# An MoE layer on one core: four residual scratches and buffers, gathers two blocks ahead

## The chip, the cores and the metric

One core of one Trainium2 chip. The metric is device time in microseconds of one execution; its median over repeated runs is compared. All data is fp32.

## The reference, cut to what matters

One transformer layer for 1024 prompt tokens and 64 sample tokens (D = 1024). First an attention and gMLP sub-layer, whose result is added to x; then a mixture of experts, which is what the change touches:

```python
p_group = softmax(t @ w_router_group + b_router_group)
g_prob, g_idx = top_k(p_group, 1)                    # one of 4 groups
logit_e = (t @ w_router_expert + b_router_expert)[group g_idx]
e_prob, e_idx = top_k(softmax(logit_e), 2)           # two of its 8 experts
weight = g_prob * e_prob / sum(e_prob)
hid = silu(xblk @ w_gate[e]) * (xblk @ w_up[e])      # blocks of 128 token slots, one expert each
yb  = hid @ w_down[e]
y   = zeros(T, D).at[row_token].add(yb * row_weight)
x   = x + gate * y
```

Each token has two slots, so two rows are added to its residual row x, in two different blocks. Both of its experts belong to one group. 2176 slots go to 32 experts (D_EXPERT = 256), 68 on average.

## The kernel before

Three stages follow each other, separated by semaphores on which all engines wait (s_end1, s_end2): projections of nine row tiles; attention, out projection, residual and router for the nine tiles; then the experts. In the second stage SyncE stores for each tile (store_tail, L542) the residual rows x_att into every residual scratch in z_d (L547), and h2, the experts' input, into ffn_input_scratch (L549). Before it loads x_att again for the tile two later it waits until those stores have landed (L652).

**Routing.** VectorE works out the slot of each token, with some help of TensorE, and writes tables of indices, `ids`: for each block b a column with the token of each of the 128 slots (TOKEN), the rows to be written if this is the token's first of two blocks (FIRST), and the output rows if it is its last (PROMPT_ROW, SAMPLE_ROW). An index that is FAR beyond the bound is skipped by the DMA. Two counts of s_tab tell that TOKEN and then all tables are there (L1948, L1961). Meanwhile GpSimd clears xg and acc (L776, L777), and SyncE loads the first four experts' weights.

**The blocks.** Block b < 32 belongs to expert `b % NG * EG + b // NG`, so to group b % 4; NG = 4, EG = 8, NE = 32. Blocks 0 to 31 hold the first 128 slots of each expert. Block 32 (NS = NE + 1 = 33 blocks are always run) takes the 128 slots after those of the first expert that has more, and further ones run in a loop only where there are more (overflow_blocks, L117); here there are none.

- **TensorE**: for block b, transposes of hid (hT4, L1178), gate and up matmuls of block b+1 (gu, L1168; L1173 and L1175), transposes of the tokens of block b+2 (xT4, L1159), then down matmuls of b (down, L1184; L1190). Transposes are recorded at line 853. down(b) waits for VectorE's copy hidT(b) (L1982) and until the down banks of b-1 have been read.
- **SyncE**: loads the 3 MB of weights of block b+4 into the slot of b once down(b) is done (L669 to L671, four slots).
- **ScalarE**: half of the xT copies (L1429), silu (L1436), and the prompt gate times row weight (L1443).
- **VectorE**: for block b, in this order (steady, L2005): hidT(b) (L1982), gate_w (L1988), hidden(b+1) (L1974), xT half of b+2 (L1966), then add_rows(b) (L1991): yb = down bank times gate (L1997), then acc += yb (L2000), which waits for the gather of residual rows of b. What stands behind that add in its queue is hidT(b+1).
- **GpSimd** issues all indirect DMAs. A residual scratch holds the partial sum of a token between its two blocks. For block b it issues, in this order (loop at L803):

```
tokens(b+4)                wait: transposes of block b+2        L783
rows_in(b+1)               wait: scatters of block b-1 landed   L786
first_rows_out(b)          wait: add of block b                 L789
last_rows_out(b), two DMAs (prompt rows, sample rows)           L792, L793
```

There are two scratches, used by even and odd blocks, and two acc buffers. Two consecutive blocks of the same parity may hold the same tokens (group b % 4 has parity b % 2); no two blocks of different parity do. Block 32 may belong to any group, so it gathers twice into acc[0]: from z_d[0] with indices EVEN, ahead of the add of block 31, and from z_d[1] with indices ODD behind the scatters of block 31 (L818 to L821); the group that isn't its own has only indices that are skipped.

Of the kernel before, what the change touches and what calls it, by code (L numbers as in the profile page):

```python
# [135 lines left out]
def build_in(nc, a, o, ctx):  # L136
    def sem(name):
        return nc.alloc_semaphore(name)
# [34 lines left out]
    tok_id = sb("tok_id", [P, NT + 1])  # L173
    TOKEN, EVEN, ODD, FIRST, PROMPT_ROW, SAMPLE_ROW = range(6)
    ids = sb("ids", [P, 6, NB], I32)
    roww = sb("roww", [P, 2, NB])
# [97 lines left out]
    yb = sb("yb", [P, D])  # L274
    gi = sb("gi", [P, 6], I32)
# [24 lines left out]
    idf = sb("idf", [P, NB])  # L300
    odd = sb("odd", [P, MAXOV])
    odd_i = sb("odd_i", [P, MAXOV], I32)
    tokf = sb("tokf", [P, 2, NT + 1])
# [26 lines left out]
    s_lss = sem("latent_square_sums_ready")  # L330
    s_rx = sem("router_exponents_ready")
    s_ry = sem("router_exponentials_ready")
    s_A1 = sem("mix_scale_ready")
# [163 lines left out]

    s_E = sem("expert_one_hots_ready")
    s_rank = sem("ranks_ready")
    s_hot = sem("slot_one_hots_ready")  # L500
    s_tabp = sem("tables_summed")
    s_tab = sem("tables_ready")
    s_gmp = sem("gate_rows_filled")
    s_gmr = sem("gate_rows_read")
    s_wd = [sem(f"expert_weights_loaded{i}") for i in range(SLOTS)]
# [12 lines left out]
    s_yv = sem("down_read")  # L518
    s_acc = [sem(f"residual_rows_gathered{i}") for i in range(2)]
    s_sum = sem("rows_summed")  # L520
    s_zsc = [sem(f"residual_rows_scattered{i}") for i in range(2)]
    s_ysc = sem("output_rows_scattered")
# [30 lines left out]
    def _(sp):  # L553
# [101 lines left out]
        store_tail(sp, LAST)  # L655
        for i in range(2):
            sp.wait_ge(s_st2[f"x2_{i}"], 32 * len(range(i, len(seq), 2)))
        sp.wait_ge(s_st2["h2"], 16 * len(seq))
# [36 lines left out]
    def _(g):  # L695
# [88 lines left out]

        def rows_in(par, z, idx):
            g.indirect_dma_start(acc[:, par], None, z, U(idx), bounds_check=TOK - 1, oob_is_err=False).then_inc(s_acc[par], 16)  # L786

        def first_rows_out(par, z, idx):
            g.indirect_dma_start(z, U(idx), acc[:, par], None, bounds_check=TOK - 1, oob_is_err=False).then_inc(s_zsc[par], 16)  # L789

# [6 lines left out]
        tokens(1, at(TOKEN, 1))  # L797
        rows_in(0, z_d[0], at(TOKEN, 0))
        for b in (2, 3):
# [26 lines left out]
        def overflow(j):  # L826

            for z in z_d:
                first_rows_out(0, z, gi[:, FIRST:FIRST + 1])
            g.wait_ge(s_zsc[0], j * 32 + 16 * (NE // 2))  # L830
            g.sem_inc(s_over, 1)
# [5 lines left out]
            rows_in(0, z_d[0], gi[:, EVEN:EVEN + 1])  # L837
            g.wait_ge(s_acc[0], j * 32 + (16 * (NE // 2 + 2) - 16))
            g.sem_inc(s_over, 1)
            rows_in(0, z_d[1], gi[:, ODD:ODD + 1])  # L840
# [10 lines left out]
    def _(pe):  # L851
# [283 lines left out]
        for v in range(2):  # L1135
# [6 lines left out]
            ins.then_inc(s_gmp, 1)  # L1142
        pe.wait_ge(s_E, 1)
        flat = E[:].rearrange("p t e -> p (t e)")
        mm(psum[0][:, 0:(NT + 1) * NE], tri[:], flat, start=True, stop=True)
        mm(psum[1][:, 0:(NT + 1) * NE], ones[:], flat, start=True, stop=True).then_inc(s_rank, 1)

        for k in range(2):
            pe.wait_ge(s_hot, k + 1)
# [4 lines left out]
        ins.then_inc(s_tabp, 1)  # L1154

# [71 lines left out]
    def _(act):  # L1227
# [185 lines left out]
        for v in range(2):  # L1413
# [3 lines left out]
            act.sem_inc(s_gmr, 1)  # L1417
        act.wait_ge(s_rx, 1)
        do(A(rt[:, 1, :, 0:NG], rt[:, 0, :, 0:NG], ACT.Exp))
        do(A(rt[:, 3, :, 0:1], rt[:, 2, :, 0:1], ACT.Exp))  # L1420
        act.sem_inc(s_ry, 1)

# [50 lines left out]
    def _(dve):  # L1473
# [386 lines left out]
        do(TT(col(2), col(11), col(8), ALU.subtract))  # L1860
        signal(s_rx)
        g4 = bcast(T(4, NG).unsqueeze(3), [P, NTT, NG, EG])
# [3 lines left out]
        do(TT(E[:], E1[:], E2[:], ALU.add))  # L1866
        signal(s_E)

        dve.wait_ge(s_ry, 1)
        do(V.tensor_reduce(col(12), T(1, NG), AXX, ALU.add))  # L1870
# [4 lines left out]

        dve.wait_ge(s_rank, 1)
        do(V.tensor_copy(big2[:], psum[1][:, 0:NTT * NE].rearrange("p (t e) -> p t e", e=NE)))
# [41 lines left out]
        for kk in range(2):  # L1919
# [4 lines left out]
            do(TT(hot, hot, bcast(tokf[:, kk, :].unsqueeze(2), [P, NTT, NB]), ALU.mult))  # L1924
            signal(s_hot)

# [13 lines left out]
        dve.wait_ge(s_tabp, 1)  # L1940
        coded, weight = psum[2][:, 0:NB], psum[2][:, NB:2 * NB]
# [63 lines left out]
        def steady(b, u, nth):  # L2005
# [3 lines left out]
            xT_half(b + 2)  # L2009
            add_rows(b, u % 2, u % 2, nth)  # L2010

        for b in range(SLOTS):
            steady(b, b, 16 * (b // 2 + 1))
        with dve.Fori(0, (NE - 2 * SLOTS) // SLOTS) as i:
            for u in range(SLOTS):
                steady(i * SLOTS + (SLOTS + u), u, i * 32 + (16 * (u // 2) + 48))
        for b in range(NE - SLOTS, NS):
# [4 lines left out]
            if b + 2 < NS:  # L2022
                xT_half(b + 2)
            add_rows(b, b % 2, b % 2, 16 * (b // 2 + 1 + (b == NE)))
        n_ov = dve.value_load(ovf_i[0:1, MAXOV:MAXOV + 1], min_val=0, max_val=MAXOV)
        def overflow(j):
# [4 lines left out]
            gate(b, 0)  # L2031
            add_rows(b, 0, 0, j * 32 + 16 * (NE // 2 + 2))

# [36 lines left out]
```

## Time and profile before

| | us |
|---|---|
| median of 3 runs | 1262.55 |
| the runs | 1262.55, 1269.23, 1247.44 |
| the profiled execution, its own time | 1251.21 |
| its span, first to last instruction | 1249.4 |
| granted TensorE clock, mean | 0.93 |
| busy in the span: TensorE, VectorE, GpSimd, ScalarE | 1082.9, 629.0, 309.6, 267.6 |

The page and the rows below are of the profiled execution. Engines: PE is TensorE (PEld its weight loads), DVE VectorE, ACT ScalarE, POOL GpSimd, SP SyncE; a trailing q is the engine's sequencer, which waits and issues. An indirect DMA's busy time on POOL is its issue alone; "to landing" is from the issue until all of it has been written. What stands in square brackets at a row's end is the idle time before it and what ended it.

### The profile page before, as it was taken

To read this page: it belongs to the slowest core of one execution; us is meant where nothing else is said; L and a number is where in the kernel's file an instruction comes from. 1 tells how busy PE (TensorE), PEld (TensorE's weight loads), DVE (VectorE), ACT (ScalarE), POOL (GpSimd) and SP (SyncE) were. 2 spreads that over 40 slices of the span, in tenths; PEclk is the share of its full clock that TensorE was granted. 3 is DMA by queue.
4 is the path that set the end of the run, shared out by engine and by line. 5 is a ranking of instruction groups with operands and counts; after the bars stand their busy time and mean duration, and the time that the engine had idled before them with its cause. 6 is when DMAs were issued, how large, how long until landed. Compare 5 with 4: busy or idle time off the path is not lost.

```text
span 1249.4 us, 13972 instructions
## 1 busy us (share of the span) xinstructions
PE 1082.9 (87%) x4732; PEld 694.4 (56%) x4732; DVE 629.0 (50%) x1209; ACT 267.6 (21%) x595; POOL 309.6 (25%) x350
## 2 busy tenths in 40 slices
PE   4699999999287989989999994399899988988993
PEld 1245555544154456657666753377677766766772
DVE  2445556554463565566575636725344334433442
ACT  1142232222233223232223201011111111111120
POOL 1122222222401110110110001124345334335443
PEclk9799999999678999999999995599999998998998
DMA  8874443331331122221120116538889887877850
GB/s 323 327 264 163 159 154 142 121 121 44 112 91 60 47 90 100 82 97 52 59 93 1 68 51 265 222 101 327 326 296 351 309 310 282 327 277 286 326 208 25
DMA packets 73200, 220.40 MB, mean 176 GB/s; under 512 B 27172, under 2 KB 30903, under 8 KB 57399
## 3 DMA queue, kind: packets, MB, share of 16 engines
q1 hardware_dynamic: 46000, 189.57, 40.4%
q0 software_dynamic: 23760, 26.81, 6.6%
q10 hardware_dynamic: 3382, 3.32, 0.8%
q8 instruction: 29, 0.48, 0.2%
q14 instruction: 29, 0.23, 0.1%
HBM read 200.04 MB, written 79.34 MB: 224 GB/s over the span
## 4 chain that ended last, share of the span: by engine, by line
PE 60%; DMA 14%; DVE 12%; issue 6%; POOL 4%; ACT 3%; ACTq 0%; DVEq 0%; POOLq 0%; SPq 0%
PE bank L898 14%; DMA out<-acc,ids 10%; PE bank L1056 8%; PE bank L853 7%; PE bank L1173 5%; PE bank L1190 5%; PE bank L1175 5%; PE bank L1007 4%; PE bank L1032 4%; DMA acc<-residual_scratch,ids 2%; PE bank L979 2%; PE bank L881 2%; DMA rope_q<-rope_table 1%; DVE probT L1767 1%; PE bank L1078 1%
## 5 line engine op out<-in xcount | busy, mean ns | idle before, releaser
L898 PE MATMUL bank<-W_in,hT 128*128 128x512 f32 (+3 forms) x432 | 181.9, 575 | 3.4 <-ACTq L1289 3.4
L718 POOL TENSOR_SCALAR st<-st 128x1 f32<-128x1 f32 (+6 forms) x77 | 17.7, 230 | 611.7 <-DVEq L1485 611.7
L1190 PE MATMUL bank<-WD,hidT 128*128 128x512 f32 x264 | 129.5, 637 | 27.8 <-DVE hidT L1982 27.8
L1056 PE MATMUL bank<-W_out,mT 128*128 128x512 f32 (+1 forms) x288 | 138.7, 614 | 2.9 <-DVEq L1479 2.9
L898 PEld LDWEIGHTS bank<-W_in,hT 128*128 128x128 f32 (+1 forms) x432 | 80.1, 188 | 94.8 <-issue 89.2
L1173 PE MATMUL bank<-WG,xT 128*128 128x256 f32 x528 | 122.5, 386 | 1.3 <-ACT xT L1429 0.8
L1175 PE MATMUL bank<-WU,xT 128*128 128x256 f32 x528 | 119.4, 379 | 0.0
L1173 PEld LDWEIGHTS bank<-WG,xT 128*128 128x128 f32 x528 | 99.9, 194 | 14.6 <-ACT xT L1429 1.2
L1175 PEld LDWEIGHTS bank<-WU,xT 128*128 128x128 f32 x528 | 100.5, 190 | 13.5
L1190 PEld LDWEIGHTS bank<-WD,hidT 128*128 128x128 f32 x264 | 51.5, 206 | 83.0 <-issue 79.8
L1032 PEld LDWEIGHTS bank<-vall,probT 128*128 128x128 f32 (+1 forms) x656 | 78.1, 187 | 23.3 <-issue 18.5
L1767 DVE COPY probT<-bank 128x512 f32<-128x512 f32 (+3 forms) x104 | 57.0, 548 | 64.9 <-PE bank L853 57.2
L1056 PEld LDWEIGHTS bank<-W_out,mT 128*128 128x128 f32 (+1 forms) x288 | 53.0, 189 | 62.7 <-issue 54.5
L786 POOL DMA_INDIRECT acc<-residual_scratch,ids x34 | 41.5, 1219 | 186.5 <-DMA out<-acc,ids 157.8
L1007 PE MATMUL bank<-kT,qT 104*128 104x512 f32 (+4 forms) x224 | 86.3, 499 | 0.7 <-ACTq L1383 0.7
L1997 DVE TENSOR_TENSOR yb<-bank,gate_w 128x512 f32<-128x512 f32 x66 | 42.5, 686 | 84.1 <-PE bank L1190 84.1
L1032 PE MATMUL bank<-vall,probT 128*128 128x64 f32 (+1 forms) x656 | 81.2, 269 | 2.9 <-DVEq L1479 2.9
L2000 DVE TENSOR_TENSOR acc<-acc,yb 128x1024 f32<-128x1024 f32 x33 | 40.4, 1225 | 80.1 <-DMA acc<-residual_scratch,ids 79.4
L1443 ACT ACTIVATE gate_w<-gate_m,roww 128x1024 f32<-128x1024 f32 x33 | 37.8, 1148 | 171.4 <-DVE yb L1997 171.4
L719 POOL TENSOR_TENSOR st<-st,mhalf 128x1 f32<-128x1 f32 (+6 forms) x77 | 70.0, 909 | 6.4
L853 PE MATMUL bank<-ident,prob 128*128 128x128 f32 (+2 forms) x328 | 49.2, 276 | 16.4 <-ACT prob L1394 6.8
L1974 DVE TENSOR_TENSOR hid<-sg,bank 128x256 f32<-128x256 f32 x33 | 20.0, 606 | 76.5 <-ACT sg L1436 76.0
(280 smaller groups left out, 1401.7 us busy)
## 6 DMA issues: line engine op xcount, KB each, us to landing
WG<-in_w_gate_e SPq DMA_DIRECT2D x33, 1024.0 KB, 6.7
WU<-in_w_up_e SPq DMA_DIRECT2D x33, 1024.0 KB, 8.9
WD<-in_w_down_e SPq DMA_DIRECT2D x33, 1024.0 KB, 12.4
ada_w<-in_w_ada SPq DMA_DIRECT2D x24, 1024.0 KB, 7.4
residual_scratch<-x_att SPq DMA_DIRECT2D x16, 512.0 KB, 3.4
kbuf<-k_scratch SPq DMA_DIRECT2D x12, 384.0 KB, 5.3
xbuf<-in_x_prompt SPq DMA_DIRECT2D x8, 512.0 KB, 3.7
W_in<-in_w_in SPq DMA_DIRECT2D x2, 2048.0 KB, 17.8
```

The costliest lines, as they stand in the source:

```text
L719: g.tensor_tensor(dst, dst, mhalf[:dst.shape[0], 0:dst.shape[1]], ALU.pow).then_inc(s_rs, 1)
L786: g.indirect_dma_start(acc[:, par], None, z, U(idx), bounds_check=TOK - 1, oob_is_err=False).then_inc(s_acc[par], 16)
L853: tr = lambda out, in_, r: nc.tensor.transpose(out, in_, ident[:r, :r])
L898: ins = mm(ps[:R, 0:n], hT[:, t % 2, k, :R], W_in[:, k, c0:c0 + n], start=(k == 0), stop=(k == KD - 1))
L1007: ins = mm(out[:R, 0:m], qT[:depth, s % 2, h, :R], kT[:depth, h, k0 + c0:k0 + c0 + m], start=True, stop=True)
L1032: ins = mm(psum[7][:R, h * VD:(h + 1) * VD], probT[:r, u % 2, b, :R], vall[:r, slot0(t) + b, h * VD:(h + 1) * VD], start=(b == 0), stop=(b ...
L1056: ins = mm(psum[6][:R, :], mT[:, k, :R], W_out[:, k, half * 512:(half + 1) * 512], start=(k == 0), stop=(k == KD - 1))
L1173: mm(psum[2][:, 0:DE], xT[:, k, :], WG[:, slot, k, :], start=(k == 0), stop=(k == KD - 1))
L1175: ins = mm(psum[3][:, 0:DE], xT[:, k, :], WU[:, slot, k, :], start=(k == 0), stop=(k == KD - 1))
L1190: ins = mm(psum[5 + half][:], hidT[:, k, :], WD[:, slot, k, half * 512:(half + 1) * 512], start=(k == 0), stop=(k == 1))
L1767: ops.append(V.tensor_copy(probT[:, u % 2, 4 * j:4 * j + len(full), :R], src[:, 0:len(full), :R]))
L1997: V.tensor_tensor(yb[:, c], psum[5 + half][:], gate_w[:, par, c], ALU.mult).then_inc(s_yv, 1)
```

## The change

One residual scratch and one acc buffer for each expert group, so four of each. Block b uses scratch, buffer and semaphores b % 4. The gather of residual rows is issued two blocks ahead (rows_in(b+2) in the step of block b; blocks 0 and 1 before the loop), and waits for the scatters of block b-2, the last before it in the same buffer. The scratch it reads was last written by block b-2, four blocks before b+2. last_rows_out(b) has a new wait, for the output scatters of block b-1. Block 32 gathers from all four scratches, one after another, each waiting for the landing of the one before: the first in the step of block 30, the second in that of 31, the third and fourth in its own, the fourth also behind the landing of block 31's scatter. The tables EVEN and ODD become four, one for each group. The second stage stores each residual tile four times instead of two. Some semaphores are joined (those of the routing stage), with the same waits.

```diff
-    z_d = [nc.dram_tensor(f"residual_scratch{i}", (TOK, D), F32).ap() for i in range(2)]
+    z_d = [nc.dram_tensor(f"residual_scratch{i}", (TOK, D), F32).ap() for i in range(NG)]
-    acc = sb("acc", [P, 2, D])
+    acc = sb("acc", [P, NG, D])
...
-                sp.wait_ge(s_st2[f"x2_{s % 2}"], 32 * (s // 2))
+                sp.wait_ge(s_st2[f"x2_{s % 2}"], 16 * NG * (s // 2))
...
         tokens(1, at(TOKEN, 1))
-        rows_in(0, z_d[0], at(TOKEN, 0))
+        rows_in(0, 0, at(TOKEN, 0))
+        rows_in(1, 1, at(TOKEN, 1))
...
-            if b:
-                g.wait_ge(s_zsc[(b - 1) % 2], 16 * ((b - 1) // 2 + 1))
-                g.wait_ge(s_ysc, 32 * b)
-            if b + 1 < NE:
-                rows_in((b + 1) % 2, z_d[(b + 1) % 2], at(TOKEN, b + 1))
-            if b + 1 == NE:
-                rows_in(0, z_d[0], at(EVEN, NE))
+            if b >= 2:
+                g.wait_ge(s_zsc[(b - 2) % NG], 16 * ((b - 2) // NG + 1))
+                g.wait_ge(s_ysc, 32 * (b - 1))
+            if b + 2 < NE:
+                rows_in((b + 2) % NG, (b + 2) % NG, at(TOKEN, b + 2))
+            if b + 2 >= NE and b + 2 - NE < NG:
+                group = b + 2 - NE
+                if group:
+                    g.wait_ge(s_acc[0], 16 * (NE // NG + group))
+                rows_in(0, group, at(GROUP + group, NE))
+            if b == NE:
+                g.wait_ge(s_zsc[NG - 1], 16 * (NE // NG))
+                g.wait_ge(s_acc[0], 16 * (NE // NG + NG - 1))
+                rows_in(0, NG - 1, at(GROUP + NG - 1, NE))
             g.wait_ge(s_sum, b + 1)
             if b < NE:
-                first_rows_out(b % 2, z_d[b % 2], at(FIRST, b))
-            last_rows_out(b % 2, at(PROMPT_ROW, b), at(SAMPLE_ROW, b))
-            if b + 1 == NE:
-                g.wait_ge(s_zsc[1], 16 * (NE // 2))
-                g.wait_ge(s_acc[0], 16 * (NE // 2 + 1))
-                rows_in(0, z_d[1], at(ODD, NE))
+                first_rows_out(b % NG, b % NG, at(FIRST, b))
+            if b:
+                g.wait_ge(s_ysc, 32 * b)
+            last_rows_out(b % NG, at(PROMPT_ROW, b), at(SAMPLE_ROW, b))
...
-        do(V.tensor_copy(odd_i[:], ovf[:, 0:MAXOV]))
-        do(TS(odd_i[:], odd_i[:], 1, None, ALU.bitwise_and))
-        do(V.tensor_copy(odd[:], odd_i[:]))
+        do(V.scalar_tensor_tensor(ovg[:], thr[:], float(-NG), ovf[:, 0:MAXOV], ALU.mult, ALU.add))
...
-        do(STT(ids[:, EVEN, NE:], odd[:], FAR, idf[:, NE:], ALU.mult, ALU.add))
-        do(TS(odd[:], odd[:], -FAR, FAR, ALU.mult, ALU.add))
-        do(TT(ids[:, ODD, NE:], odd[:], idf[:, NE:], ALU.add))
+        for group in range(NG):
+            do(TS(other[:], ovg[:], float(group), FAR, ALU.not_equal, ALU.mult))
+            do(TT(ids[:, GROUP + group, NE:], other[:], idf[:, NE:], ALU.add))
...
-            add_rows(b, u % 2, u % 2, nth)
+            add_rows(b, u % 2, u, nth)
```

## Rows read from the trace of the kernel before

**Rows 1.** The page, part 4: shares of the chain that ended last, by line.
```profile
PE bank L898 14%; DMA out<-acc,ids 10%; PE bank L1056 8%; PE bank L853 7%; PE bank L1173 5%; PE bank L1190 5%; PE bank L1175 5%; PE bank L1007 4%; PE bank L1032 4%; DMA acc<-residual_scratch,ids 2%; PE bank L979 2%; PE bank L881 2%; DMA rope_q<-rope_table 1%; DVE probT L1767 1%; PE bank L1078 1%
```

**Rows 2.** Who waited for whom after 860 us: total us, times, longest us.
```profile
POOL acc L786 <- DMA out<-acc,ids: 157.8, 25, 12.3
...
DVE acc L2000 <- DMA acc<-residual_scratch,ids: 79.4, 24, 11.3
...
PE bank L1190 <- DVE hidT L1982: 27.8, 7, 6.4
```

**Rows 3.** Timeline of GpSimd: start us, us, instruction, idle before it.
```profile
866.34 0.97 POOL L793 DMA_INDIRECT out<-acc,ids  x1 [0.30 <-PE bank L853]
...
878.39 0.97 POOL L793 DMA_INDIRECT out<-acc,ids  x1 [0.30 <-issue]
...
893.02 1.00 POOL L786 DMA_INDIRECT acc<-residual_scratch,ids  x1 [12.31 <-DMA out<-acc,ids]
894.32 1.01 POOL L789 DMA_INDIRECT residual_scratch<-acc,ids  x1 [0.30 <-issue]
...
896.93 0.97 POOL L793 DMA_INDIRECT out<-acc,ids  x1 [0.30 <-issue]
...
1132.52 0.97 POOL L793 DMA_INDIRECT out<-acc,ids  x1 [0.30 <-issue]
```

**Rows 4.** Timeline of TensorE: hidden transposes and down projections, same columns.
```profile
835.17 0.38 PE L853 MATMUL bank<-ident,hid 128*128 128x128 f32 x2
...
905.22 5.94 PE L1190 MATMUL bank<-WD,hidT 128*128 128x512 f32 x8 [4.71 <-DVE hidT L1982]
...
1041.02 0.38 PE L853 MATMUL bank<-ident,hid 128*128 128x128 f32 x2
...
1098.20 0.38 PE L853 MATMUL bank<-ident,hid 128*128 128x128 f32 x2
...
1199.92 3.60 PE L1190 MATMUL bank<-WD,hidT 128*128 128x512 f32 x8
...
1214.79 0.38 PE L853 MATMUL bank<-ident,hid 128*128 128x128 f32 x2
...
1225.35 0.38 PE L853 MATMUL bank<-ident,hid 128*128 128x128 f32 x2
1228.59 3.70 PE L1190 MATMUL bank<-WD,hidT 128*128 128x512 f32 x8 [2.86 <-DVE hidT L1982]
```

**Rows 5.** Time to landing between 835 and 1200 us: of scatter L793, then of gather L786.
```profile
DMA to landing us min/median/max: 2.2/7.3/13.8
...
DMA to landing us min/median/max: 3.2/9.3/11.3
```

**Rows 6.** Window: us, PE, PEld, DVE, ACT, POOL busy, clock, DMA share, GB/s.
```profile
911.20:978.00 66.80, 66.80 (x297) 50.84 (x296) 32.60 (x42) 12.77 (x18) 29.04 (x27) 1.00 0.92 348
```

**Rows 7.** DMA issues, 911 to 979 us: count, KB each, median us to landing.
```profile
WD<-in_w_down_e SPq DMA_DIRECT2D x6, 1024.0 KB, 12.2
```

**Rows 8.** The chain of the tail, in order of time.
```profile
1233.66 3.19 DMA acc<-residual_scratch,ids
```

**Rows 9.** Timeline of all engines, end of attention and routing.
```profile
751.04 0.79 SPq L547 DMA_DIRECT2D residual_scratch<-x_att  x2
...
756.60 0.32 SPq L549 DMA_DIRECT2D ffn_input_scratch<-h  x1
...
763.18 0.20 DVE L1730 TENSOR_TENSOR logits<-bank,b_r 128x36 f32<-128x36 f32 x1 [3.78 <-PE bank L1078]
...
765.35 1.80 POOL L777 MEMSET acc<- 128x2048 f32 x1
...
769.26 0.20 DVE L1857 TENSOR_SCALAR rt<-rt 128x72 f32<-128x72 f32 x1
...
806.05 0.17 DVE L1960 TENSOR_TENSOR ids<-odd,idf 128x16 int32<-128x16 f32 x1
...
810.88 0.69 DVE L1966 COPY xT<-bank 128x512 f32<-128x512 f32 x1 [4.66 <-PE bank L853]
```

More of the change, by code:

```diff
@@ L173, in build_in @@
     tok_id = sb("tok_id", [P, NT + 1])
-    TOKEN, EVEN, ODD, FIRST, PROMPT_ROW, SAMPLE_ROW = range(6)
-    ids = sb("ids", [P, 6, NB], I32)
+    TOKEN, FIRST, PROMPT_ROW, SAMPLE_ROW, GROUP = range(5)
+    KINDS = GROUP + NG
+    ids = sb("ids", [P, KINDS, NB], I32)
     roww = sb("roww", [P, 2, NB])
@@ L300, in build_in @@
     idf = sb("idf", [P, NB])
-    odd = sb("odd", [P, MAXOV])
-    odd_i = sb("odd_i", [P, MAXOV], I32)
+    ovg = sb("ovg", [P, MAXOV])
+    other = sb("other", [P, MAXOV])
     tokf = sb("tokf", [P, 2, NT + 1])
@@ L495, in scores @@
         return 2 * (u % 2)
[L498 to L501, printed above, removed]
+    s_hots = sem("routing_exponents_then_expert_then_slot_one_hots_ready")
+    s_sums = sem("ranks_then_tables_summed")
     s_tab = sem("tables_ready")
     s_gmp = sem("gate_rows_filled")
-    s_gmr = sem("gate_rows_read")
+    s_gmr = sem("gate_rows_read_then_router_exponentials_ready")
     s_wd = [sem(f"expert_weights_loaded{i}") for i in range(SLOTS)]
@@ L518, in build_in @@
     s_yv = sem("down_read")
-    s_acc = [sem(f"residual_rows_gathered{i}") for i in range(2)]
+    s_acc = [sem(f"residual_rows_gathered{i}") for i in range(NG)]
     s_sum = sem("rows_summed")
-    s_zsc = [sem(f"residual_rows_scattered{i}") for i in range(2)]
+    s_zsc = [sem(f"residual_rows_scattered{i}") for i in range(NG)]
     s_ysc = sem("output_rows_scattered")
@@ L656, in _ @@
         for i in range(2):
-            sp.wait_ge(s_st2[f"x2_{i}"], 32 * len(range(i, len(seq), 2)))
+            sp.wait_ge(s_st2[f"x2_{i}"], 16 * NG * len(range(i, len(seq), 2)))
         sp.wait_ge(s_st2["h2"], 16 * len(seq))
@@ L783, in tokens, with rows_in, first_rows_out @@
             g.indirect_dma_start(xg[:, par], None, h2_d, U(idx), bounds_check=TOK - 1, oob_is_err=False).then_inc(s_xg[par], 16)
[L785 to L789, printed above, removed]
+        def rows_in(k, group, idx):
+            g.indirect_dma_start(acc[:, k], None, z_d[group], U(idx), bounds_check=TOK - 1, oob_is_err=False).then_inc(s_acc[k], 16)
+        def first_rows_out(k, group, idx):
+            g.indirect_dma_start(z_d[group], U(idx), acc[:, k], None, bounds_check=TOK - 1, oob_is_err=False).then_inc(s_zsc[group], 16)
         def last_rows_out(par, prompt_idx, sample_idx):
@@ L826, in overflow @@
         def overflow(j):
[L828 to L831, printed above, removed]
+            for group in range(NG):
+                first_rows_out(0, group, gi[:, FIRST:FIRST + 1])
+            for group in range(NG):
+                g.wait_ge(s_zsc[group], j * 16 + 16 * (NE // NG))
+                g.sem_inc(s_over, 1)
             g.wait_ge(s_xTp, j + NE)
@@ L836, in overflow @@
             tokens(0, gi[:, TOKEN:TOKEN + 1])
[L837 to L840, printed above, removed]
+            for group in range(NG):
+                rows_in(0, group, gi[:, GROUP + group:GROUP + group + 1])
+                g.wait_ge(s_acc[0], j * (16 * NG) + 16 * (NE // NG + group + 1))
+                g.sem_inc(s_over, 1)
             g.wait_ge(s_sum, j + (NE + 1))
@@ L1142, in _ @@
             ins.then_inc(s_gmp, 1)
-        pe.wait_ge(s_E, 1)
+        pe.wait_ge(s_hots, 2)
         flat = E[:].rearrange("p t e -> p (t e)")
         mm(psum[0][:, 0:(NT + 1) * NE], tri[:], flat, start=True, stop=True)
-        mm(psum[1][:, 0:(NT + 1) * NE], ones[:], flat, start=True, stop=True).then_inc(s_rank, 1)
+        mm(psum[1][:, 0:(NT + 1) * NE], ones[:], flat, start=True, stop=True).then_inc(s_sums, 1)
         for k in range(2):
-            pe.wait_ge(s_hot, k + 1)
+            pe.wait_ge(s_hots, k + 3)
             for t in range(NT + 1):
@@ L1153, in _ @@
                          start=(t == 0 and k == 0), stop=(t == NT and k == 1))
-        ins.then_inc(s_tabp, 1)
+        ins.then_inc(s_sums, 1)
         pe.wait_ge(s_gmr, 2)
@@ L1417, in _ @@
             act.sem_inc(s_gmr, 1)
-        act.wait_ge(s_rx, 1)
+        act.wait_ge(s_hots, 1)
         do(A(rt[:, 1, :, 0:NG], rt[:, 0, :, 0:NG], ACT.Exp))
         do(A(rt[:, 3, :, 0:1], rt[:, 2, :, 0:1], ACT.Exp))
-        act.sem_inc(s_ry, 1)
+        act.sem_inc(s_gmr, 1)
         do(A(sg[0:1, 0:1], ident[0:1, 0:1], ACT.Silu))
@@ L1860, in _ @@
         do(TT(col(2), col(11), col(8), ALU.subtract))
-        signal(s_rx)
+        signal(s_hots)
         g4 = bcast(T(4, NG).unsqueeze(3), [P, NTT, NG, EG])
@@ L1866, in _ @@
         do(TT(E[:], E1[:], E2[:], ALU.add))
-        signal(s_E)
-        dve.wait_ge(s_ry, 1)
+        signal(s_hots)
+        dve.wait_ge(s_gmr, 3)
         do(V.tensor_reduce(col(12), T(1, NG), AXX, ALU.add))
@@ L1874, in _ @@
         do(TT(col(15), col(14), col(3), ALU.mult))
-        dve.wait_ge(s_rank, 1)
+        dve.wait_ge(s_sums, 1)
         do(V.tensor_copy(big2[:], psum[1][:, 0:NTT * NE].rearrange("p (t e) -> p t e", e=NE)))
@@ L1939, in _ @@
         do(V.tensor_copy(ovf_i[:], ovf[:]))
-        dve.wait_ge(s_tabp, 1)
+        dve.wait_ge(s_sums, 2)
         coded, weight = psum[2][:, 0:NB], psum[2][:, NB:2 * NB]
@@ L1957, in _ @@
         do(STT(ids[:, SAMPLE_ROW, :], number[:], float(-SEQ - 1), far[:], ALU.add, ALU.add))
-        do(STT(ids[:, EVEN, NE:], odd[:], FAR, idf[:, NE:], ALU.mult, ALU.add))
-        do(TS(odd[:], odd[:], -FAR, FAR, ALU.mult, ALU.add))
-        do(TT(ids[:, ODD, NE:], odd[:], idf[:, NE:], ALU.add))
+        for group in range(NG):
+            do(TS(other[:], ovg[:], float(group), FAR, ALU.not_equal, ALU.mult))
+            do(TT(ids[:, GROUP + group, NE:], other[:], idf[:, NE:], ALU.add))
         signal(s_tab)
@@ L2023, in _ @@
                 xT_half(b + 2)
-            add_rows(b, b % 2, b % 2, 16 * (b // 2 + 1 + (b == NE)))
+            add_rows(b, b % 2, b % NG, 16 * (b // NG + (NG if b == NE else 1)))
         n_ov = dve.value_load(ovf_i[0:1, MAXOV:MAXOV + 1], min_val=0, max_val=MAXOV)
@@ L2031, in overflow @@
             gate(b, 0)
-            add_rows(b, 0, 0, j * 32 + 16 * (NE // 2 + 2))
+            add_rows(b, 0, 0, j * (16 * NG) + 16 * (NE // NG + NG))
         overflow_blocks(dve, n_ov, overflow)
```

10 lines of the change are left out of this document (4 added, 6 removed).

## The prediction, made before the change was run

> **What bounds the kernel now.** I read the chain that ended last first, since it says what the end waits for. By line, the first entry is a matmul of the projections, and the second, 10% of the span or 125 us, is no engine's work but the landing of the output scatters (DMA out<-acc,ids); with 2% for the landing of the residual gathers, the only entries of the expert loop beside its matmuls, 5% for each of L1173, L1175 and L1190 [rows 1]. So the change is worth what the expert loop loses to those landings.
>
> The waits after 860 us give its links in order [rows 2]. GpSimd sits 157.8 us before its gathers of residual rows (L786) until the output scatters of the block before have landed. VectorE sits 79.4 us before its add (L2000) until that gather has landed. TensorE sits 27.8 us, in 7 pieces, before down projections (L1190) until VectorE, held in its queue by that add, has copied hidT. Only the last is on the path.
>
> GpSimd's timeline shows one lap. The scatter L793 of one block starts at 878.39, the gather that waits for its landing at 893.02, and the next L793 at 896.93 [rows 3]: a lap of 14.63 + 3.91 = 18.54 us. From the L793 at 866.34 to the one at 1132.52 are 20 laps, so 13.31 us each; 3.91 of that is issue, 9.40 is the wait (landing, the issue of the token gather beside it, wake-up). TensorE needs less for a block: 1041.02 to 1098.20 is five blocks without a stall, 57.18 / 5 = 11.44 us [rows 4]. GpSimd's ring of gather, add and scatter is longer than TensorE's block, falls behind, and every few blocks VectorE, then TensorE, stand still for it.
>
> What that costs in all comes from two hidden transposes. The one of block 1 starts at 835.17, that of block 32 at 1225.35: 390.2 us for 31 blocks. At the unstalled pace it would be 30 x 11.44 and a last one of 10.56 (1214.79 to 1225.35, no token transposes): 353.6. So 36.5 us are lost. Six of the seven stalls lie in between; the seventh, 2.86 at 1228.59, stays. 27.8 - 2.9 = 24.9 us of the 36.5 is standing still; the other 11.6 is mostly the down projection after a stall, which runs slower: 5.94 us behind the first of the six against 3.60 in a block without one (905.22 and 1199.92 [rows 4]). It goes with the stalls.
>
> **The change part by part.**
> (a) Gather two blocks ahead, waiting for the scatters of block b-2 instead of b-1. Those were issued a whole block earlier, longer ago than nearly all landings (scatter at most 13.8 us, median 7.3 [rows 5]). The gather for b+2 leaves at about the time of down projection b, and the add that reads it comes at least two blocks, 22.9 us, later; it lands in 9.3 at the median and 11.3 at most [rows 5]. Some 13 us are spare. All six stalls should go: -36.5 us. What is late next is TensorE itself.
> (b) The new wait: last_rows_out(b) stands behind the landing of the output scatters of b-1. Behind it in GpSimd's queue are those scatters, the token gather for b+5 and the residual gather for b+3; VectorE waits for the latter two only through their transposes and adds, blocks later. The ring of output scatters is now: wait 9.40, one issue of 1.3 (half of 894.32 to 896.93, two issues [rows 3]), so 10.7 us a lap against 11.44. The three other issues (3.9) lie beside the landing. Bounds: with the longest wait seen a lap is 14.63 + 1.3 = 15.9; with the smallest landing, 2.2, issue alone (5 x 1.3 = 6.5) sets it. I take 10.7: the nearest rows are twenty laps of the same transfers beside the same loads. That is a margin of 0.7 us a lap, thin, and beside it the 13 us spare of (a) to absorb long ones: cost 0, range 0 to rival B.
> The same transfer with the DMA engines free shows what the loads add: the last gather lands in 3.19 us [rows 8] against 9.3. The Trainium skill, "DMA: Bandwidth & Descriptors", section "Anatomy of one DMA — SWDGE (gpsimd) path", puts a GpSimd transfer at about 2 us plus its bytes over 436 GB/s; an estimate by it for some 70 rows of 4 KB is 2.7 us, which fits the free tail and not the loop. By the rule the lap would be pure issue and rival B impossible; the trace says otherwise, so B keeps a chance.
> (c) TensorE at full pace asks for its weights faster. In a stretch of 66.8 us without a stall the DMA engines moved 348 GB/s at a share of 0.92 and clock 1.00 [rows 6]: 23.2 MB in 5.84 blocks, 3.98 MB a block. WD, the last to land of a block's three, landed in 12.2 us [rows 7], and it is asked for about three blocks (34 us) ahead. Cost 0; the other end is rival C.
> (d) The tail. Block 32 now gathers from four scratches, one after another into one buffer. The first two are issued behind blocks 30 and 31's adds and lie beside work. Before, one gather (of z1) came behind the scatters of block 31: issued 1233.66, landed 3.19 later [rows 8]. Now two come there, the second waiting for the first: another 3.2 of landing and some 0.8 for wake-up and issue. +4.0 us (bounds: 0 if the third is early enough to hide, 8 if the second group's is late too).
> (e) Four residual stores instead of two for each attention tile. The last two are issued at 751.04, h2 follows at 756.60, and the stage ends with VectorE's logits at 763.18 [rows 9]. Two more of 0.5 MB have 5.6 us to themselves before h2 is issued, and h2 then 6.6 us. Cost 0, bounds 0 to 2.
> (f) GpSimd's memset of acc doubles from 1.80 to 3.6 us and ends at 768.95, before VectorE's tensor_scalar at 769.26, and long before the tables that GpSimd waits for. Three table instructions at the end (the last at 806.05, 0.2 us apart) become eight, +1.0 us, in front of VectorE's copy at 810.88, which waits 4.66 us for TensorE [rows 9]. Three casts become one in front of a wait for TensorE. All 0. Joined semaphores issue nothing.
>
> Sum: the profiled execution took 1251.2 us (span 1249.4 and 1.8 around it). 1251.2 - 36.5 + 4.0 = 1218.7. I add 1.3 for a small stall somewhere and forecast 1220. The three runs of before have a median of 1262.55, 11 above the profiled one, and 1247.4 to 1269.2 at their ends; I take that spread to be mostly more or fewer of the same stalls, which leave with the change, so the forecast stands also for the median (if the 11 us lie elsewhere, 1231).
>
> **The rivals.**
> A, stalls that remain. The gather and scatters still share 16 busy engines with 3 MB loads; a run of long laps eats the 13 us, and half of the loss stays: 1251.2 - 18 + 4 = 1237. For it: landings vary from 2.2 to 13.8. Against: it takes many long laps in a row.
> B, slower: the output ring becomes the bound. Place: the wait in front of last_rows_out. Its cost is 31 x (wait + 1.3 - 11.44) less the spare 13, and it eats the whole gain once the wait averages (36.5 - 4.0 + 13) / 31 + 10.14 = 11.6. If two laps in three were like the longest (14.6) and one like the mean, the wait is 12.9: 31 x 2.76 - 13 = 72.6, so 1218.7 + 72.6 = 1291. For it: with TensorE never pausing, the DMA engines never get their rest. Against: twenty laps averaged 9.4 with that traffic for most of the time.
> C, transfers bound the loop: 3.98 MB a block at 320 GB/s would be 12.4 us, 31 x 1.0 = 31 more: 1250, no gain. Against: 348 GB/s at 0.92 busy [rows 6], with WD far ahead of its use.
> D, the change doesn't remove the wait, since something else in GpSimd's queue (the token gather, the wait for the add) delays the gather as long: 1251 + 4 = 1255. Against: both come earlier than the landing in the lap of rows 3.
>
> **How the numbers follow.** Forecast 0.75, A 0.12, B 0.05, C 0.05, D 0.03. A measurement of this kernel can tell about 2% from no change, that is below 1237 against the median 1262.5. Faster by over 2%: the forecast and half of A, 0.81. Within: half of A, C, D, 0.14. Slower: B, 0.05. The range: below, 1218.7 with the tail hidden and the lowest run's 4 us taken off, 1209; above, the forecast with the 11 us elsewhere and part of A, 1240. About 0.2 lies outside.
>
> **What would show it.** Right: TensorE's waits for hidT shrink from seven to about one; VectorE's wait for the gather goes from 79 to near the tail's; the two hidden transposes stand 354 us apart; L792 now waits on "DMA out", some laps, in total well under 157.8 us; a second serial gather at the end. Wrong: GpSimd laps above 11.44 us between L793s (B), TensorE or its loads waiting for weights (C), gathers still starting late (D), or attention ending later than 763 us (e).

## The result, and the profile after

| | before | after |
|---|---|---|
| median | 1260.13 us (4 runs, 1247.4 to 1269.2) | 1219.62 us (4 runs, 1218.2 to 1225.1) |
| ratio | 1 | 0.9714, 95% interval 0.9672 to 0.9756 |
| the profiled execution, and its span | 1251.21, 1249.4 | 1218.23, 1216.5 |
| TensorE clock in the profiled execution | 0.930 | 0.937 |

Faster by 2.9%. The forecast was 1220 us. The two profiled executions differ by 33.0 us; the sum of the prediction, before its allowance of 1.3, said 32.5. The medians differ by 40.5, since the profiled execution of before was one of the faster ones. Here and below, ratios and their intervals leave out a run that is over 1.5% above the fastest of its kernel.

First the chain that ended last, from part 4 of the page of the changed kernel, by engine and by line, to be held against [rows 1]. (The same instruction has a line number that is up to 3 lower or 4 higher than before, and up to 10 off in the kernels of the experiments: the output scatters are L789 and L790, the residual gather L783, the token gather L780 in the changed kernel and in those made from it.)

```profile
PE 76%; DVE 12%; issue 3%; ACT 3%; DMA 2%; POOL 2%; ACTq 1%; DVEq 0%; POOLq 0%; SPq 0%
PE bank L902 15%; PE bank L1177 10%; PE bank L1179 9%; PE bank L1194 9%; PE bank L1060 9%; PE bank L857 8%; PE bank L1011 5%; PE bank L1036 4%; PE bank L983 2%; PE bank L885 2%; DVE probT L1771 1%; PE bank L1082 1%; POOL st L716 1%; PE bank L869 1%; PE bank L912 1%
```

The landing of output scatters, 10% before, is off the list; the three matmul lines of the expert loop have gone from 5% each to 9 or 10. The chain now runs along TensorE through the loop.

Who waited for whom after 860 us (total us, times, longest us), against [rows 2]:

```profile
POOL out L789 <- DMA out<-acc,ids: 108.8, 23, 5.8
...
DVE acc L2002 <- DMA acc<-residual_scratch,ids: 4.4, 1, 4.4
...
PE bank L1194 <- DVE hidT L1984: 2.9, 1, 2.9
```

Of TensorE's seven waits for hidT one is left, that of block 32; of VectorE's 79.4 us before the gather, 4.4 in the tail. GpSimd still waits long for output scatters, 108.8 us against 157.8, but now in front of the next ones (L789). TensorE's timeline shows the same from its side: the hidden transposes of blocks 1 and 32, and the down projections of block 31 and 32.

```profile
834.83 0.38 PE L857 MATMUL bank<-ident,hid 128*128 128x128 f32 x2
...
1185.06 3.60 PE L1194 MATMUL bank<-WD,hidT 128*128 128x512 f32 x8
1188.49 0.38 PE L857 MATMUL bank<-ident,hid 128*128 128x128 f32 x2
1191.73 5.40 PE L1194 MATMUL bank<-WD,hidT 128*128 128x512 f32 x8 [2.86 <-DVE hidT L1984]
```

From 834.83 to 1188.49 are 353.7 us, against 390.2 in [rows 4] and 353.6 forecast for a loop without stalls. Behind 1188.49 come 28.0 us of span, against 24.05 (1249.4 - 1225.35) before. Both large terms are to be read off these rows: 36.5 gained, 4.0 given back.

A step of GpSimd in the middle of the loop (start us, us, instruction, idle before it), against [rows 3]:

```profile
1009.27 0.99 POOL L789 DMA_INDIRECT out<-acc,ids  x1 [4.89 <-DMA out<-acc,ids]
1010.56 1.28 POOL L790 DMA_INDIRECT out<-acc,ids  x1 [0.30 <-issue]
1012.15 1.04 POOL L780 DMA_INDIRECT xg<-ffn_input_scratch,ids  x1 [0.31 <-issue]
1013.49 1.00 POOL L783 DMA_INDIRECT acc<-residual_scratch,ids  x1 [0.30 <-issue]
1014.80 1.01 POOL L786 DMA_INDIRECT residual_scratch<-acc,ids  x1 [0.30 <-issue]
1020.75 0.98 POOL L789 DMA_INDIRECT out<-acc,ids  x1 [4.94 <-DMA out<-acc,ids]
1022.04 1.34 POOL L790 DMA_INDIRECT out<-acc,ids  x1 [0.30 <-issue]
```

From L790 to L790 it is 11.48 us: 10.2 until the next output scatter may start, 1.3 for one issue. All five issues of a step lie in it, and L786 doesn't wait for the add, which had ended 5.6 us before, at 1009.2: GpSimd runs late, held by the new wait. The output scatter L789 of that block leaves at 1020.75, when the add of the next block ends. The landing of L790 between 835 and 1170 us, then that of the gather L783:

```profile
DMA to landing us min/median/max: 5.8/9.3/14.8
```

```profile
DMA to landing us min/median/max: 7.1/9.2/15.8
```

Against [rows 5] the scatter's median has gone from 7.3 to 9.3 us and the gather's is as it was. The windows (us, then busy time of PE, PEld, DVE, ACT and POOL, clock, DMA share, GB/s) show that the loop no longer pauses; in the same two stretches of the kernel before it was 317 and 294 GB/s at shares of 0.85 and 0.78.

```profile
880.00:960.00 80.00, 80.00 (x351) 60.20 (x350) 38.03 (x49) 14.93 (x21) 38.19 (x32) 1.00 0.92 346
960.00:1040.00 80.00, 80.00 (x351) 60.18 (x350) 38.02 (x49) 14.92 (x21) 37.57 (x35) 1.00 0.92 352
```

The busier DMA engines aren't what made the landing longer: in the unstalled stretch of [rows 6], at the same 348 GB/s and share of 0.92, the kernel before landed the same scatters in 6.2 us at the median. What the landing goes with is seen when it is put beside the weight loads. The last load of a block, WD, issued at 1007.91, and its time to landing; then that of the scatter L790 issued at 1010.56:

```profile
1007.91 0.38 SPq L668 DMA_DIRECT2D WD<-in_w_down_e  x1
...
DMA to landing us min/median/max: 11.8/11.8/11.8
```

```profile
DMA to landing us min/median/max: 9.4/9.4/9.4
```

The weights are there at 1019.7, the scattered rows at 1019.9. One block on, WD issued at 1019.25 takes 12.1 us and the scatter issued at 1022.04 takes 9.5: 1031.3 and 1031.5. From block 13 to block 27 fourteen of fifteen last output scatters land 0.2 us behind the WD of the load then in flight. Those loads are issued when a down projection is done, so once every block of TensorE; a ring whose scatter lands with them takes that pace, and that is how the lap comes to be 11.48 us, as far as the rows show it.

The chain of the tail, in order of time, against [rows 8]:

```profile
1196.73 2.14 DMA acc<-residual_scratch,ids
1198.88 0.02 issue
...
1199.73 3.09 DMA acc<-residual_scratch,ids
```

Two gathers stand one behind the other where one stood. They cost 2.8 of the 4.0 us: the add of block 32 starts 14.4 us behind the hidden transposes of block 32, against 11.6 before. The rest, 1.1 us, stands behind that add: from the landing of the last output scatter to the end of the span it is 7.7 us (1208.8 to 1216.5) against 6.5 (1242.9 to 1249.4). No instruction is recorded there, and its cause stays open. Last, the end of attention and of routing, against [rows 9]:

```profile
750.60 2.86 SPq L544 DMA_DIRECT2D residual_scratch<-x_att  x4
...
762.73 0.20 DVE L1734 TENSOR_TENSOR logits<-bank,b_r 128x36 f32<-128x36 f32 x1 [3.78 <-PE bank L1082]
...
764.91 3.51 POOL L774 MEMSET acc<- 128x4096 f32 x1
```

```profile
768.82 0.20 DVE L1861 TENSOR_SCALAR rt<-rt 128x72 f32<-128x72 f32 x1
...
810.67 0.69 DVE L1968 COPY xT<-bank 128x512 f32<-128x512 f32 x1 [3.84 <-PE bank L857]
```

Four stores instead of two, and the stage ends at the same distance behind them (12.1 us, as before). The longer memset ends at 768.42 and the next tensor_scalar starts on time, 6.1 us behind the logits in both. VectorE's idle time in front of its copy is 0.8 shorter, which took up most of the added table instructions: behind the logits the copy starts 0.2 us later than before, the hidden transposes of block 1 0.1 us.

### The profile page after: what moved, and what is told of

It is laid out like the page before. It is cut to its first block, busy times and chain, and to the rows that moved or that the text cites. A ratio compares the mean times of both kernels' runs of the same rounds, so it can differ in the third digit from the quotient of the medians.

```text
span 1216.5 us, 13997 instructions
## 1 busy us (share of the span) xinstructions
PE 1069.6 (88%) x4732; PEld 688.8 (57%) x4732; DVE 629.5 (52%) x1212; ACT 267.9 (22%) x595; POOL 322.5 (27%) x352
## 4 chain that ended last, share of the span: by engine, by line
PE 76%; DVE 12%; issue 3%; ACT 3%; DMA 2%; POOL 2%; ACTq 1%; DVEq 0%; POOLq 0%; SPq 0%
PE bank L902 15%; PE bank L1177 10%; PE bank L1179 9%; PE bank L1194 9%; PE bank L1060 9%; PE bank L857 8%; PE bank L1011 5%; PE bank L1036 4%; PE bank L983 2%; PE bank L885 2%; DVE probT L1771 1%; PE bank L1082 1%; POOL st L716 1%; PE bank L869 1%; PE bank L912 1%
## 5 line engine op out<-in xcount | busy, mean ns | idle before, releaser
L1194 PE MATMUL bank<-WD,hidT 128*128 128x512 f32 x264 | 120.6, 600 | 2.9 <-DVE hidT L1984 2.9
L1194 PEld LDWEIGHTS bank<-WD,hidT 128*128 128x128 f32 x264 | 48.2, 192 | 51.6 <-issue 48.5
L789 POOL DMA_INDIRECT out<-acc,ids x33 | 34.9, 1057 | 115.7 <-DMA out<-acc,ids 108.8
L780 POOL DMA_INDIRECT xg<-ffn_input_scratch,ids x33 | 36.8, 1114 | 69.4 <-DVEq L1483 35.5
## 6 DMA issues: line engine op xcount, KB each, us to landing
WD<-in_w_down_e SPq DMA_DIRECT2D x33, 1024.0 KB, 12.1
```

The source lines that it names most:

```text
L1194: ins = mm(psum[5 + half][:], hidT[:, k, :], WD[:, slot, k, half * 512:(half + 1) * 512], start=(k == 0), stop=(k == 1))
```

## The experiments

The prediction's theory has two halves that the change makes together: the ring on GpSimd (gather, add, scatter, landing, next gather) was longer than TensorE's block, and it is broken by waiting for the scatters of two blocks back; and the gather leaves a block earlier. Four kernels take these apart; the others ask what makes the ring long, how near its edge the new one is, and what the additional scratches cost.

**Back in the ring.** Four scratches and buffers stay; the order of issue is the old one, and only block 0's gather stands before the loop.

```diff
-            if b >= 2:
-                g.wait_ge(s_zsc[(b - 2) % NG], 16 * ((b - 2) // NG + 1))
-                g.wait_ge(s_ysc, 32 * (b - 1))
-            if b + 2 < NE:
-                rows_in((b + 2) % NG, (b + 2) % NG, at(TOKEN, b + 2))
+            if b:
+                g.wait_ge(s_zsc[(b - 1) % NG], 16 * ((b - 1) // NG + 1))
+                g.wait_ge(s_ysc, 32 * b)
+            if b + 1 < NE:
+                rows_in((b + 1) % NG, (b + 1) % NG, at(TOKEN, b + 1))
...
-            if b:
-                g.wait_ge(s_ysc, 32 * b)
             last_rows_out(b % NG, at(PROMPT_ROW, b), at(SAMPLE_ROW, b))
```

> The changed kernel with four scratches and four buffers kept, but the gather again one block ahead and behind the landing of the scatters of the block before; the wait in front of the output scatters is then covered and taken out. Theory 'ring' (the prediction's): what cost 36.5 us was the ring on GpSimd of gather, add, scatter, landing; it is back, so laps of 13.3 us between output scatters, six or so stalls of TensorE, and 1219.6 + 36.5 = 1256 (1245 to 1268). Rival 'room': the additional scratches and buffers themselves brought the gain, the order of issue nothing: 1220.

Measured: 1263.4 us (10 runs, 1255.3 to 1276.5), ratio to before 1.0018 (0.9972 to 1.0065). All of the gain is gone. Its waits after 860 us:

```profile
POOL acc L783 <- DMA out<-acc,ids: 153.4, 25, 12.1
...
DVE acc L1999 <- DMA acc<-residual_scratch,ids: 80.9, 21, 11.2
...
PE bank L1191 <- DVE hidT L1981: 27.8, 6, 6.2
```

They are those of [rows 2] to a few us, and the hidden transposes of blocks 1 and 32 stand 389.4 us apart (1226.89 - 837.51), against 390.2 before. Scratches and buffers alone bring nothing: "room" is out.

**Two ahead, but in the ring.** Gathers keep the lead; each step begins with the wait for the scatters of b-1, ahead of the token gather and the residual gather, and the two later waits are gone.

```diff
         for b in range(NS):
+            if b:
+                g.wait_ge(s_zsc[(b - 1) % NG], 16 * ((b - 1) // NG + 1))
+                g.wait_ge(s_ysc, 32 * b)
             if b + 4 < NS:
                 g.wait_ge(s_xTp, b + 3)
                 tokens(b % 2, at(TOKEN, b + 4))
-            if b >= 2:
-                g.wait_ge(s_zsc[(b - 2) % NG], 16 * ((b - 2) // NG + 1))
-                g.wait_ge(s_ysc, 32 * (b - 1))
...
-            if b:
-                g.wait_ge(s_ysc, 32 * b)
             last_rows_out(b % NG, at(PROMPT_ROW, b), at(SAMPLE_ROW, b))
```

> Gathers stay two blocks ahead, but each step of GpSimd begins with the wait for the landing of the scatters of the block before, ahead of its five issues. Theory 'ring': a lap is then landing 7.3 to 9.3 + 0.9 wake-up + four issues of 1.3 before the next last scatter, 13.4 to 15.4 against TensorE's 11.44; by the formula of rival B, 31 x (13.4 - 11.44) - 13 = 48 more, 1268 (1255 to 1300). Rival 'lead': only that the gather leaves two blocks ahead matters, and landings fit themselves to the pace: 1220, laps of 11.44.

Measured: 1304.6 us (1298.8 to 1312.4), ratio to before 1.037 (1.027 to 1.047). It is slower than before by 3.7%, with its gathers two blocks ahead, and slower than the 1255 to 1300 that the ring theory gave. A step of GpSimd here:

```profile
1000.46 0.97 POOL L790 DMA_INDIRECT out<-acc,ids  x1 [0.30 <-issue]
1010.02 1.59 POOL L780 DMA_INDIRECT xg<-ffn_input_scratch,ids  x1 [8.59 <-issue]
1011.92 1.43 POOL L783 DMA_INDIRECT acc<-residual_scratch,ids  x1 [0.31 <-issue]
1013.65 1.02 POOL L786 DMA_INDIRECT residual_scratch<-acc,ids  x1 [0.30 <-issue]
1014.97 0.99 POOL L789 DMA_INDIRECT out<-acc,ids  x1 [0.30 <-issue]
1016.27 0.98 POOL L790 DMA_INDIRECT out<-acc,ids  x1 [0.31 <-issue]
```

9.6 us until the landing is seen and 6.3 of issues make a lap of 15.8. It is one of the longer ones: from block 3 to block 28 the laps are 14.8 us on average, within the 13.4 to 15.4 expected, and the hidden transposes of blocks 1 and 32 stand 428.8 us apart, 75 more than in the changed kernel. With such laps the lead of a block is used up once, and afterwards TensorE goes at the ring's pace. Lead doesn't replace pace: "lead" is out. Its waits show who runs dry first:

```profile
PE bank L855 <- DMA xg<-ffn_input_scratch,ids: 48.2, 15, 5.0
```

Not the residual rows: VectorE waits for those once, 9.3 us. It is the token gather, which stands in the same queue behind the same wait.

**One ahead, out of the ring.** The gather for b+1 again in step b, but behind the scatters of b-2. Output scatters get one semaphore for even and one for odd blocks, so that wait needs no other beside it.

```diff
-                g.wait_ge(s_ysc, 32 * (b - 1))
-            if b + 2 < NE:
-                rows_in((b + 2) % NG, (b + 2) % NG, at(TOKEN, b + 2))
+                g.wait_ge(s_ysc[b % 2], 32 * (b // 2))
+            if b + 1 < NE:
+                rows_in((b + 1) % NG, (b + 1) % NG, at(TOKEN, b + 1))
...
-            if b:
-                g.wait_ge(s_ysc, 32 * b)
-            last_rows_out(b % NG, at(PROMPT_ROW, b), at(SAMPLE_ROW, b))
+            last_rows_out(b % NG, b, at(PROMPT_ROW, b), at(SAMPLE_ROW, b))
```

> The gather for block b+1 in step b (one ahead), behind the landing of the scatters of b-2; two semaphores for output scatters, so no wait in front of them. Theory 'ring': the landing is out of the ring, and the gather has one block and a down projection and yb, 11.44 + 3.4 + 1.3 = 16 us, for a landing of 9.2 at the median and 15.8 at most: 1220 to 1226, with VectorE's wait for the gather small. Rival 'lead': the second block of lead is what brings it; with one, late gathers stall often, half of the loss or more is back: 1238 or over.

Measured: 1219.4 us (1216.3 to 1221.4), ratio to before 0.968 (0.959 to 0.977): the time of the whole change. Its waits after 860 us:

```profile
DVE acc L2000 <- DMA acc<-residual_scratch,ids: 52.1, 23, 4.5
```

VectorE does wait for most gathers, 2.3 us on average, and TensorE not once for it in the loop, which takes 353.7 us. So the second block of lead isn't what gained the time; it only makes these short waits go.

**No wait in front of the output scatters.** The changed kernel with the two semaphores, gathers two ahead, the new wait gone.

> The changed kernel without the wait in front of the output scatters: two semaphores for them, even and odd blocks, gathers two ahead behind the landing of b-2. Theory 'ring': that wait (108.8 us of GpSimd's time in the changed kernel) costs the end nothing: 1218 to 1221. Rival 'queue': the wait delays gathers by up to 5.8 us each and is worth some us, 1214 or less. Rival 'contention': without it more transfers lie in flight beside the weight loads, landings grow, 1225 or more.

Measured: 1220.9 us (1218.1 to 1223.7). The same as with it, in spite of 108.8 us of waiting there. GpSimd now keeps up with VectorE:

```profile
POOL residual_scratch L786 <- DVE acc L2001: 94.3, 28, 5.8
...
POOL acc L783 <- DMA out<-acc,ids: 22.6, 10, 3.9
```

Neither "queue" nor "contention" shows in the time. That landings grow without the wait is so, though: in the pair of kernels with one scratch, further down, the token gather lands in 13.3 us at the median without it and in 8.9 with it (870 to 1150 us), the residual gather in 14.8 and 9.6. With gathers two blocks ahead that costs nothing.

**Why landings take so long.** The kernel before the change, with lighter loads: of WU's 1 MB only an eighth is loaded from block 4 on. What it computes is therefore not the layer any more; the routing, and so the tables and every DMA of GpSimd, are the same.

```diff
-            sp.dma_start(WU[:, slot], w["w_up_e"][0, bass.ds(e, 1)].rearrange("o (p k) n -> (o p) k n", k=KD)).then_inc(s_wd[slot], 16)
+            sp.dma_start(WU[:, slot, 0:1], w["w_up_e"][0, bass.ds(e, 1)].rearrange("o (p k) n -> (o p) k n", k=KD)[:, 0:1]).then_inc(s_wd[slot], 16)
```

> The kernel before the change, with a reload of WU that brings 128 KB of its 1 MB from block 4 on (the other rows keep an earlier expert's weights): 28% of the loop's load bytes are gone, and no instruction or wait of GpSimd is touched. Theory: landings of 7 to 9 us are long because the scatters share the DMA engines with the loads; without a part of them they land in some 5, the lap of 13.3 falls under 11.44, TensorE's stalls go: 1263 - 36.5 = 1226, near 1215 on the scale of the changed kernel (1215 to 1232). Rival: landings are a fixed cost of an indirect scatter, and the stalls stay: 1250 to 1263.

Measured: 1214.3 us (1211.6 to 1215.8), ratio to before 0.961 (0.954 to 0.967). Its wait for output scatters after 860 us, and the landing of the token gather L783 from 835 to 1200 us (8.6 us at the median in the same stretch of the kernel before):

```profile
POOL acc L786 <- DMA out<-acc,ids: 72.8, 21, 4.6
```

```profile
DMA to landing us min/median/max: 3.9/5.1/5.9
```

Without a line of GpSimd's program changed, the longest wait falls from 12.3 to 4.6 us, the hidden transposes of blocks 1 and 32 stand 353.7 us apart, and the runs spread over 4 us instead of 16. The DMA engines moved 266 to 276 GB/s at a share of 0.78 to 0.79 here. The ring was long because its transfers ran beside 3 MB of loads a block; whether they were held in the DMA engines or at the memory behind them isn't separated.

**How near the edge the new ring is.** The new wait one instruction earlier.

```diff
             g.wait_ge(s_sum, b + 1)
+            if b:
+                g.wait_ge(s_ysc, 32 * b)
             if b < NE:
                 first_rows_out(b % NG, b % NG, at(FIRST, b))
-            if b:
-                g.wait_ge(s_ysc, 32 * b)
             last_rows_out(b % NG, at(PROMPT_ROW, b), at(SAMPLE_ROW, b))
```

> The changed kernel with its new wait one instruction earlier, in front of first_rows_out instead of in front of the output scatters: one more issue of 1.3 us on the ring of output scatters. Theory 'ring with landings of their own': landing 9.3 + 0.9 + 2 x 1.3 = 12.8 a lap against 11.44, of which the spare of the gathers takes 8 us: 31 x 1.36 - 8 = 34 more, 1254 (1235 to 1265). Rival 'landings fit themselves to the pace', since they end with a block's loads: the lap stays 11.44, 1220.

Measured: 1225.4 us (1220.3 to 1226.3), ratio to before 0.974 (0.969 to 0.980), against 0.971 for the changed kernel on the same chip. Both expectations fail, the first (1254) by far, the second (1220, laps of 11.44) by 5 us. The loop is 7.2 us longer than 353.7, in three late token gathers, of which the last, with the idle time in front, is

```profile
1145.67 1.89 PE L857 MATMUL bank<-ident,xg 128*128 128x128 f32 x8 [3.98 <-DMA xg<-ffn_input_scratch,ids]
```

So 1.3 us more on the ring costs some 7 us and not 34. The landing of the last output scatter in this kernel is 8.0 us at the median, 1.3 less than in the changed one: issued later, it still lands with the loads, 0.4 to 1.0 us behind WD in ten laps running (blocks 14 to 23). Landings are not a fixed price; here they end where a block's loads end. The hold isn't perfect: laps from block 14 to 26 are 11.75 us on average, so this ring does fall behind, slowly, until token gathers are late.

**One scratch.** Since blocks of different groups hold different tokens, one scratch will do with four buffers and the same waits. Block 32 then gathers once, and attention stores its rows once.

```diff
-    z_d = [nc.dram_tensor(f"residual_scratch{i}", (TOK, D), F32).ap() for i in range(NG)]
+    z_d = [nc.dram_tensor("residual_scratch", (TOK, D), F32).ap()]
...
-            if b + 2 >= NE and b + 2 - NE < NG:
-                group = b + 2 - NE
-                if group:
-                    g.wait_ge(s_acc[0], 16 * (NE // NG + group))
-                rows_in(0, group, at(GROUP + group, NE))
             if b == NE:
                 g.wait_ge(s_zsc[NG - 1], 16 * (NE // NG))
-                g.wait_ge(s_acc[0], 16 * (NE // NG + NG - 1))
-                rows_in(0, NG - 1, at(GROUP + NG - 1, NE))
+                rows_in(0, 0, at(TOKEN, NE))
```

> The changed kernel itself, on the chip of the three that follow, so that a few us can be told: 1219.6 as measured before (1218 to 1225).

> One residual scratch instead of four, with the four buffers and the order of the changed kernel: blocks of different groups hold different tokens, so a gather still has to wait only for its own group's scatters. Block 32 gathers once, behind block 31's scatter; each attention tile stores its residual rows once. Theory of the prediction: only the tail is shorter, by the serial gather it was said to add, landing 3.1 and 0.8: 1219.6 - 4 = 1215.6. Rival: the tail's gathers lie beside down projection 32 and its reading, so one fewer saves under 1 us: 1219. Rival on step (e): the three stores fewer for a tile are worth something too, 1213 or less.

Measured: the changed kernel again 1218.5 us (6 runs, 1217.8 to 1221.3), with one scratch 1216.1 (1212.2 to 1225.4); ratios to before 0.9705 (0.9665 to 0.9745) and 0.9690 (0.9642 to 0.9737). The medians differ by 2.4 us, but the intervals overlap. In the profiled executions the span behind the hidden transposes of block 32 is 28.0 us in the one and 24.9 in the other, and the chain of the second has one gather there:

```profile
1196.61 3.29 DMA acc<-residual_scratch,ids
```

The loop is 353.7 us in both, and block 1's hidden transposes start at 835.12 and 834.73. So step (d) is shown in place, at 3.1 us in all, of which 2.9 stand before the last add, the size of the serial gather; 0.9 of the 4.0 us stays with one scratch too. Step (e) costs nothing beyond 0.4.

**One scratch, and no wait in front of the output scatters.**

> The kernel before this one, with two semaphores for output scatters and no wait in front of them. If that wait is free: the same time as with it, 1215.6. If GpSimd, a block late by it, is at the edge of what the gathers bear, fewer bad runs: the median the same, the highest of the runs lower (under 1220).

Measured: 1217.0 us (6 runs, 1214.1 to 1219.7), ratio 0.9682 (0.9642 to 0.9722). The wait is free here too. The highest run is lower, as expected, but 1225.4 was one run of six, which shows little. Both one-scratch kernels beat the one before the change clearly and the changed one by 1.5 and 2.4 us, which is at the edge of what can be told.

## Why the prediction was right

- **What bounds (the ring, 36.5 us).** Right in mechanism and size: 36.5 us went. Shown from both sides: the old order with all the new memory gives 1263.4, lighter loads under the old order take the stalls away. The 11.6 us that the prediction gave to slower down projections are the granted clock: it was 0.61 in the one of 5.94 us behind the first stall and between 0.58 and 0.69 in the five that took 5.2 to 6.3 us; behind the sixth stall, of 2.35 us, it was 1.00 and the down projection took 3.70. The six together took 10.6 us more than six of 3.60. The first of them, and one without a stall (same columns as the windows above):

```profile
905.20:911.10 5.90, 5.88 (x9) 2.54 (x10) 2.58 (x3) 0.00 (x0) 3.14 (x4) 0.61 0.27 85
...
1199.90:1203.50 3.60, 3.60 (x12) 1.64 (x11) 1.11 (x2) 0.60 (x1) 0.84 (x1) 1.00 0.62 257
```

- **(a) Two blocks ahead.** The prediction put the two halves of the edit into one step and named the lead first. What gained the time is the other half, waiting for two blocks back: one ahead with that wait is as fast (1219.4), two ahead without it is slower than before (1304.6). The spare of 13 us was also reckoned for the residual gather, whereas the token gather behind the same waits is what runs out first.
- **(b) The new wait, cost 0.** Right in cost (1220.9 without it), wrong in its margin. A lap was put at 10.7 us; it is 11.48, TensorE's own pace, as the scatters land with the weight loads of the block. The 0.7 us of margin a lap were not there, and output scatters leave some 9 us later behind their add than in the first blocks (11.5 us, 1009.2 to 1020.75, against 2.9). What kept the ring at TensorE's pace without that margin is its tie to the loads, which the prediction didn't have: in this term the 0 is in part luck. Rival B's formula, with the wait as an independent number, overstates: one more issue on the ring was to cost 34 us and cost 7. As to the mechanism, B is real: laps of 14.8 on average bring 1304.6.
- **The rule of the Trainium skill** ("DMA: Bandwidth & Descriptors", "Anatomy of one DMA — SWDGE (gpsimd) path", 2 us plus bytes over 436 GB/s, by which a landing would be 2.7 us): the run with lighter loads goes its way, 5.1 us for the token gather instead of 8.6, but doesn't reach it. The traces come near it only where no loads are in flight (gathers of 3.1 and 3.3 us in the tails, the last output scatters 2.3 to 2.8). Beside loads at a share of 0.92 the measurement decides.
- **(c) Weights.** Right: 346 to 352 GB/s at clock 1.00, and TensorE waited for none.
- **(d) Tail +4.0.** +3.95 in the span, but the match is luck in part: the second gather cost 2.8 us instead of 4.0, and 1.1 us came behind the last scatter, where the prediction had put nothing.
- **(e) and (f), 0.** Right; the memset was 3.51 instead of 3.6.
- **The spread of the runs of before.** Taken to be stalls. Without the runs left out it was 15.1 us before, 6.9 with the change and 4 with lighter loads; the old order in new memory had 15.1 again. That fits, and on it rests that the forecast held for the median too, but no run of before other than the profiled one has a trace, and with one scratch six runs spread over 13 us.
- **The allowance of 1.3** for a small stall: there was none in the profiled execution, so rival A did not occur, nor did D, as gathers started early enough.
- **The lower end of the range.** 1218.7 with the tail hidden (4.0) and the lowest run's 3.8 us taken off is 1210.9, not 1209. Nothing hangs on it.

## What to carry to other kernels

A step that waits for its own last transfer before it issues the next is a ring, and its length, landing plus all issues behind the wait, stands against the block time of the bounding engine. Prefetching by one more block doesn't shorten it; moving the wait to a transfer one block older, at the price of more buffers, does. (More scratches were not needed for it: one did as well as four.) Count everything that is queued behind the wait, not only the transfer that it is for. And look at what a landing ends with before using it as a number: a median from a stretch that was just as busy gave 6.2 us here for what took 9.3, because the landing went with other loads and not with its own length.

## What had not been expected

- Landings and pace hang together. In the profiled execution GpSimd's wait in front of L789 settled between 3.9 and 5.8 us, mostly at 4.5 to 5.0, for some twenty laps, with TensorE at full pace; in a second one of the same kernel it waited there only 14 times, 58.7 us in all, and the loop took the same 353.7. Putting one more issue (1.3 us) into the ring shortened the median landing from 9.3 to 8.0. The rows above show that the scatters land with the loads; by what means, no run here tells, and it doesn't hold everywhere: with one scratch and no wait in front of the output scatters, they land mostly 5 to 6.5 us behind a block's WD from block 14 on.
- A down projection behind a stall of TensorE of 3.9 to 6.4 us took 5.2 to 6.7 us instead of 3.6, in the kernel before and in that of the first experiment; behind three stalls of 2.4 to 3.0 us two took 3.7 and one 5.4. The granted clock goes with it in the kernel before: 0.58 to 0.69 in the long ones, 1.00 in the one of 3.7. So a stall costs nearly half as much again: 24.9 us of standing still were 36.5 in all.
